# Expert stage of a two-block network: larger VectorE quotas per up round, and 20 instead of 4 gelu rows kept in SBUF

## What is computed

```python
def _peer(h, wq, keys, u, v):
    q = (hb @ wq).reshape(tc, PEER_HEADS, 2, PEER_HALF)
    s = jnp.einsum('thpk,hpnk->thpn', q, keys)
    s_top, i_top = lax.top_k(s, PEER_TOPK)
    cand = s_top[:, :, 0, :, None] + s_top[:, :, 1, None, :]
    best, pos = lax.top_k(cand.reshape(tc, PEER_HEADS, -1), PEER_TOPK)
    eid = jnp.take_along_axis(cid.reshape(tc, PEER_HEADS, -1), pos, -1)
    g = jax.nn.softmax(best)
    act = jax.nn.gelu(jnp.einsum('td,thed->the', hb, u[eid]), approximate=False)
    return jnp.einsum('the,thed->td', g * act, v[eid])
```

## Time and profile of the kernel before

| what | us |
|---|---|
| median of 3 runs | 3786.34 (3786.01 to 3790.39) |
| time of the profiled execution | 3789.86 |
| span of the profile | 3787.8 |
| up rounds of the changed stage, from the first gelu to the last | 489 to 1208.8 |
| pause until the first down product | 1208.8 to 1232.3 |
| down rounds | 1232.3 to 1791 |
| until the next stage starts | 1791 to 1807.8 |

### The profile page before, as it was taken

The page is one execution under the profiler, slowest core; times in us unless marked ns, Lnnn a source line. Parts: engine busy times, 40 slices in busy tenths (PEclk is TensorE's granted clock), DMA queues, the critical chain, the costliest instruction groups (busy, mean ns, idle before and its releaser), DMA issues. The chain is left out here.

```text
span 3787.8 us, 56067 instructions
## 1 busy us (share of the span) xinstructions
PE 3556.8 (94%) x21807; PEld 3153.1 (83%) x21807; DVE 2732.2 (72%) x5456; ACT 1689.3 (45%) x3029; POOL 395.3 (10%) x282
## 2 busy tenths in 40 slices
PE   7999999999997999998699999999997899989899
PEld 5777998999897877887577999998886888988798
DVE  4557366878786888888546797778887767766775
ACT  4344233555554333333434444443334535564554
POOL 0000000000454343343200000000000000000000
PEclk9999999999999999999899999999998999999999
DMA  5133366544899999998213575556665213442243
GB/s 229 63 132 133 114 244 253 186 168 167 324 352 346 332 390 365 369 381 310 85 51 145 184 231 186 167 184 229 251 242 187 112 72 146 181 169 90 83 173 139
DMA packets 181767, 773.02 MB, mean 204 GB/s; under 512 B 22976, under 2 KB 70592, under 8 KB 131584
## 3 DMA queue, kind: packets, MB, share of 16 engines
q1 hardware_dynamic: 144640, 635.20, 46.3%
q0 software_dynamic: 36864, 134.23, 9.4%
HBM read 699.38 MB, written 69.99 MB: 203 GB/s over the span
## 5 line engine op out<-in xcount | busy, mean ns | idle before, releaser
L2907 DVE TENSOR_TENSOR expert_ring_low<-expert_ring,expert_high 128x1024 fp32r<-128x1024 f32 x256 | 312.9, 1222 | 169.9 <-ACT expert_high L3236 166.6
L2192 ACT ACTIVATE expert_high<-expert_ring 128x1024 fp32r<-128x1024 f32 x256 | 270.6, 1057 | 211.3 <-PE ps L2119 211.3
L1922 DVE TENSOR_TENSOR expert_ring_low<-expert_ring,expert_high 128x1024 fp32r<-128x1024 f32 x256 | 311.7, 1219 | 70.7 <-ACT expert_high L2192 70.7
L3133 PE MATMUL ps<-hidden_high,expert_high 128*128 128x384 f32 x1024 | 353.7, 345 | 0.0
L3135 PE MATMUL ps<-hidden_high,expert_ring_low 128*128 128x384 f32 x1024 | 344.2, 336 | 0.0
L3134 PE MATMUL ps<-hidden_low,expert_high 128*128 128x384 f32 x1024 | 343.8, 336 | 0.0
L3236 ACT ACTIVATE expert_high<-expert_ring 128x1024 fp32r<-128x1024 f32 x256 | 270.0, 1055 | 118.0 <-PE ps L3170 112.5
L3424 POOL DMA_INDIRECT x<-in_peer_rows,spots x128 | 181.4, 1417 | 1107.7 <-DVE spots L2979 605.0
L2088 PE MATMUL ps<-peer_hT_high_peer,expert_high 128*128 128x256 f32 x1024 | 293.9, 287 | 0.6 <-DVE expert_ring_low L1922 0.5
L2090 PE MATMUL ps<-peer_hT_high_peer,expert_ring_low 128*128 128x256 f32 x1024 | 287.0, 280 | 0.0
L2089 PE MATMUL ps<-peer_hT_low,expert_high 128*128 128x256 f32 x1024 | 287.0, 280 | 0.0
(11 more groups left out here) (777 smaller groups left out, 9762.4 us busy)
## 6 DMA issues: line engine op xcount, KB each, us to landing
expert_ring<-in_peer_u SPq DMA_DIRECT2D x128, 1024.0 KB
expert_ring<-in_peer_v SPq DMA_DIRECT2D x128, 1024.0 KB
weight_ring<-in_ffn_w_up SPq DMA_DIRECT2D x22, 2048.0 KB, 7.5
weight_ring<-in_w_in SPq DMA_DIRECT2D x14, 2048.0 KB, 7.3
weight_ring<-in_w_mod SPq DMA_DIRECT2D x12, 2048.0 KB, 7.5
mod_slot<-in_w_mod SPq DMA_DIRECT2D x12, 2048.0 KB, 10.5
pair_weights<-pair_weights_out SPq DMA_DIRECT2D x24, 1024.0 KB
gelu_first<-gelu_out SPq DMA_DIRECT2D x62, 384.0 KB
```

Of the source, the lines that this page charges most:

```text
L1922: dve.tensor_tensor(piece(low, n), piece(raw, n), high[:, n % LEAD, :].bitcast(F32), ALU.subtract).then_inc(low_done, 1)
L2192: act.activation(high[:, n % LEAD, :], piece(raw, n), ACT.Identity).then_inc(high_done, 1)
L2907: dve.tensor_tensor(self.piece(G.e_low, n), self.piece(G.e_raw, n), G.e_high[:, n % LEAD, :].bitcast(F32), ALU.subtract).then_inc(self.S.l ...
L3133: pe.matmul(o, b[:, s], B.hs[0][:, c, 0:DW], start=(c == 0), stop=False)
```

## The change

The quotas become 3900 and 3300 ns; the down quota stays at 1700 ns. `STAY` = 20 rows of gelu stay in SBUF: 4 in the ring as before (`RING`), and the last 16 in a new tensor `ge_kept` of 24 KB a partition, which takes the place of the selection's buffers. The assertion on the end of the selection follows from it. The table's input buffer `w_in` moves to where the table's staging was, and with it the load of `x_last` moves from down round 24 to down round 124, behind a wait for the last use of that buffer. The down rounds begin 16 rows of keys earlier than before, and loads of gelu begin with down round 20.

```diff
@@ -2849,7 +2849,8 @@
 PARTS = PAIRS // PART
 LAG = PART + 2
 U_SLOTS, V_SLOTS = 3, 4
-EARLY_NS, TABLE_NS, DOWN_NS = 2600, 2300, 1700
+EARLY_NS, TABLE_NS, DOWN_NS = 3900, 3300, 1700
+STAY, RING = 20, 4
 GROW_AT = 40
 
 E_SIGNALS = (
@@ -2875,7 +2876,11 @@
 
     def expert(self, r):
 
-        return (r + N_KEYS - KEPT) % N_KEYS
+        return (r + N_KEYS - STAY) % N_KEYS
+
+    def gelu_at(self, e):
+
+        return self.B.ge_out[:, e % RING, :] if e < N_KEYS - STAY + RING else self.B.ge_kept[:, e - (N_KEYS - STAY + RING), :]
 
     def scores_of(self, g):
         k, n = divmod(4 * g, 2 * PEER_HEADS)
@@ -3044,8 +3049,8 @@
     def weigh(self, dve, r):
         S, B = self.S, self.B
         n, j = self.weights_of(r)
-        m = r // 4 - 1
-        if r < KEPT:
+        m = (r - STAY) // 4
+        if r < STAY:
             dve.wait_ge(S.gelu_done, self.expert(r) + 1)
         elif r % 4 == 0:
             dve.wait_ge(self.ge_landed[m % 2], 16 * (m // 2 + 1))
@@ -3053,7 +3058,7 @@
             dve.wait_ge(self.w_landed[n % 2], 16 * (n // 2 + 1))
         if r >= 1:
             dve.wait_ge(S.aw_split, r)
-        ge = B.ge_out[:, r, :] if r < KEPT else B.ge_in[:, m % 2, r % 4, :]
+        ge = self.gelu_at(self.expert(r)) if r < STAY else B.ge_in[:, m % 2, r % 4, :]
         w = B.w_in[:, n % 2, :, j * BLOCK:(j + 1) * BLOCK]
         dve.tensor_tensor(B.aw[:, :].rearrange("p (b t) -> p b t", t=BLOCK), ge.rearrange("p (b t) -> p b t", t=BLOCK), w,
                           ALU.mult).then_inc(S.aw_done, 1)
@@ -3084,7 +3089,7 @@
             left += EARLY_NS if r < TABLES_AT - 1 else TABLE_NS
             while left > 0:
                 left -= next(pieces, left)
-        assert at["selected"] < N_KEYS - 8
+        assert at["selected"] < N_KEYS - STAY
         for r in range(2):
             self.weigh(dve, r)
             self.split_weights(dve, r)
@@ -3238,9 +3243,9 @@
     def gelu(self, act, r):
         S, p = self.S, r // 2
         act.wait_ge(S.scored, r + 1)
-        if r % 2 == 0 and p >= 2:
+        if r % 2 == 0 and 2 <= p < (N_KEYS - STAY + RING) // 2:
             act.wait_ge(self.ge_stored[p % 2], 16 * (p // 2))
-        act.activation(self.B.ge_out[:, r % 4, :], self.G.ps[:, r % 3, 0:DW], ACT.Gelu).then_inc(S.gelu_done, 1)
+        act.activation(self.gelu_at(r), self.G.ps[:, r % 3, 0:DW], ACT.Gelu).then_inc(S.gelu_done, 1)
 
     def shares(self, act, g):
         S, B = self.S, self.B
@@ -3335,14 +3340,14 @@
     def load_ge(self, sp, m):
         B = self.B
         if m >= 2:
-            sp.wait_ge(self.S.aw_done, KEPT + 4 * (m - 1))
+            sp.wait_ge(self.S.aw_done, STAY + 4 * (m - 1))
         sp.dma_start(B.ge_in[:, m % 2, :, :], B.ge_dram[:, 4 * m:4 * m + 4, :]).then_inc(self.ge_landed[m % 2], 16)
 
     def load_w(self, sp, n):
         B = self.B
         if n >= 2:
             sp.wait_ge(self.S.aw_done, self.weights_end(n - 2))
-        first = (N_KEYS - KEPT, 0)[n > 0] if n == 0 else 8 * n - 8
+        first = self.expert(0 if n == 0 else self.weights_end(n - 1))
         size = 8 if 0 < n < W_LOADS - 1 else KEPT
         sp.dma_start(B.w_in[:, n % 2, :, 0:size * BLOCK],
                      B.w_dram[:, :, first * BLOCK:(first + size) * BLOCK].rearrange("b p n -> p b n")).then_inc(self.w_landed[n % 2], 16)
@@ -3356,7 +3361,7 @@
         for p in range(UNITS_U):
             sp.wait_ge(S.scored, UJ * (p + 1))
             self.load_unit(sp, p + E_SLOTS)
-            if UJ * p < N_KEYS - KEPT:
+            if UJ * p < N_KEYS - STAY:
                 sp.wait_ge(S.gelu_done, UJ * (p + 1))
                 sp.dma_start(B.ge_dram[:, UJ * p:UJ * p + UJ, :], B.ge_out[:, UJ * p % 4:UJ * p % 4 + UJ, :]).then_inc(
                     self.ge_stored[p % 2], 16)
@@ -3372,7 +3377,7 @@
             self.store_w(sp, b)
         sp.wait_ge(S.table_ready, DT)
         for b in range(2):
-            sp.wait_ge(self.ge_stored[b], 16 * (N_KEYS - KEPT) // (2 * UJ))
+            sp.wait_ge(self.ge_stored[b], 16 * (N_KEYS - STAY) // (2 * UJ))
         self.load_ge(sp, 0)
         self.load_ge(sp, 1)
         for b in range(2):
@@ -3384,17 +3389,18 @@
             sp.wait_ge(S.pv_done, r)
             if UNITS_U + q + E_SLOTS < 2 * UNITS_U:
                 self.load_unit(sp, UNITS_U + q + E_SLOTS)
-            if q % 2 == 1 and 2 <= q // 2 + 1 < (N_KEYS - KEPT) // 4:
-                self.load_ge(sp, q // 2 + 1)
+            if r % 4 == 0 and 2 <= (r - STAY) // 4 + 1 < (N_KEYS - STAY) // 4:
+                self.load_ge(sp, (r - STAY) // 4 + 1)
             n = (r - KEPT) // 8 + 2
             if r >= KEPT and (r - KEPT) % 8 == 0 and n < W_LOADS:
                 self.load_w(sp, n)
             if r == 24:
                 sp.dma_start(B.rows_w[:, :], B.ln_w.partition_broadcast(P)).then_inc(S.rows_landed, 16)
                 sp.dma_start(B.rows_b[:, :], B.ln_b.partition_broadcast(P)).then_inc(S.rows_landed, 16)
-                sp.dma_start(B.x_last[:, :], G.x_spill[:, SPARSE, :]).then_inc(S.x_landed, 16)
                 sp.dma_start(G.front.q.raw[:, :, :], G.front.q.src).then_inc(S.q_landed, 16)
             if r == N_KEYS - E_SLOTS:
+                sp.wait_ge(S.aw_done, self.weights_end(W_LOADS - 2))
+                sp.dma_start(B.x_last[:, :], G.x_spill[:, SPARSE, :]).then_inc(S.x_landed, 16)
                 G.ws.refill(sp, S.pv_done, (N_KEYS - E_SLOTS,))
         G.ws.refill(sp, S.pv_done, (N_KEYS, N_KEYS, N_KEYS))
         sp.wait_ge(S.dotted, PAIRS)
@@ -3491,11 +3497,12 @@
     B.shift = pick.take("best_shift", [P, PEER_HEADS, 16], F32)
     B.ex = pick.take("best_exp", [P, PEER_HEADS, 16], F32)
     B.sm = pick.take("best_sum", [P, PEER_HEADS, 2], F32)
-    B.w_in = room(96, 24).take("pair_weights_in", [P, 2, BLOCKS, 8 * BLOCK], F32)
+    B.w_in = room(16, 24).take("pair_weights_in", [P, 2, BLOCKS, 8 * BLOCK], F32)
     late = room(120, 12)
     B.aw = late.take("weighted", [P, DW], F32)
     B.ah = late.take("weighted_high", [P, 3, DW], F32R)
     B.al = late.take("weighted_low", [P, 3, DW], F32R)
+    B.ge_kept = room(96, 24).take("gelu_kept", [P, STAY - RING, DW], F32)
     B.table = room(127.5, 4.5).take("pair_table", [P, 3, DW], F32)
     B.ge_out = room(132, 6).take("gelu_out", [P, 4, DW], F32)
     few = room(138, 1.75)
```

## The result

The changed kernel takes 3820.10 us (median of 4 runs, 3817.92 to 3822.68) against 3786.18 us before; the ratio is 1.0088, with a 95% interval of 1.0076 to 1.0101. It is 33.9 us slower. Forecast were 19 us, 3805, with a range up to 3832.

A forecast was written before the change was run, and what follows sets the result against it. Up rounds with table work were taken as bound by a ring through DVE and ACT, down rounds by PE unless loads are late; +18 + 3 + 8 + 8 - 18 = +19 us on 3786.3 gave 3805, range 3775 to 3832.

The forecast's parts named there:

- the forecast's own: Whole kernel: the main forecast of 3805 us, with its own range of 3790 to 3818 and chance 0.50.
- rival 1: Up rounds: gathers choke them through the DMA engines or POOL's issues, +42 us, 3828; chance 0.18.
- The pause: Between up and down rounds: its chain of last group, store and table load stays the same, 0 +-3 us.
- The ring as bound: Up rounds with table work: a DVE and ACT dependency loop sets their length, leaving 3.24 us for DVE's pieces.
- Rival 2: Up rounds: short rounds repay long ones, so the added DVE work largely vanishes, 3760 to 3776; chance 0.15.
- Rounds with three pieces: Up rounds 55 to 127: 47 rounds each exceed DVE's free time by 0.38 us, +18 us.
- ACT's shares: Up rounds: ACT's gelu of eight dots waits for DVE in 12 rounds instead of two, net +8 us.
- Selection: Up rounds to 54: more exceed the free time, one exponential less falls by table rounds, net +3 us (0 to +8).
- Gathers in the up rounds: After a start both kernels pay, 53 rounds wait for rows at 393 GB/s, +8 us (0 to 31).
- POOL: Up rounds: 2.64 gather issues of 1.70 us each stay hidden while one takes under 2.23 us.
- Down rounds: Stalls after the 48th round go, and 1 to 3 us between the 24th and 48th: -18 us (-14 to -34).

The follow-up runs named there:

- e3: Changed kernel with quotas of 3900 ns in the first 31 up rounds and 2300 ns after, as before: 3772.71 us, ratio 0.9958.
- e5: Changed kernel with quotas of 3900 and 2500 ns, so never three sparse pieces in an up round: 3770.68 us, ratio 0.9957.
- e2: Kernel before, with 4 kept rows, given only the change's quotas of 3900 and 3300 ns: 3824.82 us, ratio 1.0091.
- e7: Changed kernel with gathers of 128 instead of 1024 columns for all rows of v and the first 96 of u: 3784.91 us, ratio 0.999.
- e4: Changed kernel with ACT's gelu of eight dot products one round later: 3809.43 us, ratio 1.0048.
- e1: Changed kernel with the quotas of before (2600 and 2300 ns), leaving only the 20 kept rows and their moves: 3785.84 us, ratio 0.9992.
- e10: Kernel before (4 kept rows) with quotas of 3900 and 2500 ns and ACT's gelu of eight dots one round later: 3773.48 us, ratio 0.9966.
- e11: Changed kernel (20 kept rows) with quotas of 3900 and 2500 ns and ACT's gelu of eight dots one round later: 3770.93 us, ratio 0.9957.
- e8: Changed kernel with quotas of 4400 and 2500 ns and ACT's gelu of eight dots one round later: 3783.46 us, ratio 0.9989.

## Why the prediction was right, and where it was off

**The sum.** Measured were +33.9 us, forecast +19. The measured time lies in the stated range, but 2 us past the forecast's own (3790 to 3818) and nearer rival 1 (3828) than 3805; and a sign of rival 1 appeared, DVE idle before dots for rows (20 times, 20.2 us). The up part grew by 46.4 us (forecast 37): 29 for the quotas, as forecast, and 17 for transfers, forecast 8. The pause added 4.2, forecast at nothing.

**The ring as bound: right.** That rounds of the table are set by a ring through DVE and ACT and not by PE, that 3.24 us are free in it, and that anything beyond is paid without repayment: e3 and e5 (never three pieces) keep 712.9 and 715.1 us, e2 and the change (three in most rounds) do not. Rival 2, the ring that absorbs, is out.

**Rounds with three pieces, and ACT's shares: right in sum.** Forecast were 18 and 8 us. The intervals of low parts show 5.76 to 5.90 for plain rounds of three, 7.45 for a share behind a third piece, and 6.08 to 6.15 for ten rounds of three that also hold the product `coefs` of eight gelu, which I hadn't counted. In e7, where rows are hardly late, the up part is 26.6 us longer than before. In it the start of the gathers is gone, which had cost 4.8 us before (the round with the wait of the earlier trace rows took 10.31 us), and its own dots still wait 2.2 us: 26.6 + 4.8 - 2.2 = 29 us for the quotas, selection included, the 18 + 3 + 8 of the forecast.

**Selection: right, though its row of the table says +8.5 against +3.** The +3 set the whole selection of the kernel before, up to round 82, against the shorter one after. But a part of the old one lies behind the 55th gelu, where the row ends: one exponential (the low part of 909.87 in the earlier trace rows came 8.57 us after the one before it, 3.06 over 5.51) and two rounds with large pieces, 1.29 and 0.34 over. With these 4.7 us the selection cost +3.8, and the row below it is +42.7 on the forecast's footing, not +38.0. Here is one of the rounds that two large pieces lengthen, DVE in the changed kernel:

```profile
698.97 1.23 DVE L2912 TENSOR_TENSOR expert_ring_low<-expert_ring,expert_high 128x1024 fp32r<-128x1024 f32 x1 [0.95 <-ACT expert_high L3241]
701.25 4.60 DVE L2974 TENSOR_REDUCE selected<-one_hot 128x128 f32<-128x2048 f32 x2
705.76 1.22 DVE L2912 TENSOR_TENSOR expert_ring_low<-expert_ring,expert_high 128x1024 fp32r<-128x1024 f32 x1
```

6.79 us from one low part to the next, 1.28 more than 5.51, as the prediction's 1.25.

**Gathers in the up rounds: the term that was mis-sized.** Forecast were 8 us; e7 gives 19.8, and on the forecast's footing, with the start that the kernel before pays too, 17. The rate wasn't the error. Windows of the changed kernel (columns as in rows 1) for the 67th to the 108th gelu and for the last 20 rounds:

```profile
885.00:1133.00 248.00, 225.04 (x1311) 213.87 (x1310) 223.34 (x251) 127.67 (x295) 162.84 (x108) 0.99 1.00 389
1133.00:1257.00 124.00, 111.56 (x644) 107.48 (x643) 109.71 (x123) 63.03 (x145) 81.60 (x54) 0.96 0.94 350
```

The 374 GB/s above are an average over parts that don't fill the engines. Where the DMA share is 1.00 the rate was 389, as good as the 393 assumed. There a round took 6.06 us, forecast 6.03, and 5.85 in e7, forecast 5.90: 8.6 us for 41 rounds. The rest lies where I had put nothing. Up to the 67th gelu the changed kernel loses 8.1 us to e7, not the same start as before: with three dots in a round several waits for rows follow one another. And the last 20 rounds lose 3.2, though at a share of 0.94 the engines weren't full all the time. On the forecast's footing that is 8.1 - (4.8 - 2.2) = 5.5 for the start, 8.6 and 3.2, 17.3 in all. The step that failed is that both kernels pay the start alike and that only the mean rate counts after it.

A late row also costs a second time, in PE's clock. After the round of 9.11 us at 1077.54, in which a dot waited 2.69 us for rows, PE had idled 3.66 us before its next work; its matmuls of 384 columns took 0.52 us instead of 0.33, and a round of three took 6.73 us instead of 5.80. The granted clock of this window is a mean of the two levels, 1.2 and 2.4 GHz:

```profile
1087.00:1099.00 12.00, 9.41 (x44) 9.44 (x45) 11.33 (x13) 6.12 (x14) 7.01 (x5) 0.72 0.86 299
```

The term lay between my bounds (0 and 31). Of the ceilings that the Trainium skill gives ("DMA: Bandwidth & Descriptors", section "Measured"), neither is what these stretches show: 425 GB/s for one core alone was not reached in any total here, 358 was passed.

**POOL: right to leave out.** Counted as in the prediction, with the idle time that nothing else explains, an issue took 1.80 us for v and 1.56 for u in the changed kernel (busy 1.62 and 1.40), under the 2.23 that would have counted. With DVE busy 88% instead of 80% the issue for v was thus 0.1 us dearer (that for u was cheaper, 1.56 against 1.69), not 0.53, and e7 needed as long for an eighth of the bytes.

**Down rounds: right, -18.6 against -18**, and in the places named: 16.0 us after the 48th round (330.1 before, 314.1 now), 1.6 between the 24th and 48th, 1.0 before.

**The pause: +4.2, forecast at nothing with +-3.** SP's issue of the table's two loads took 12.80 us instead of 7.00 before:

```profile
1220.91 7.00 SPq L3347 DMA_DIRECT2D pair_weights_in<-pair_weights  x2
```

```profile
1267.71 12.80 SPq L3352 DMA_DIRECT2D pair_weights_in<-pair_weights  x2
```

```profile
1246.31 6.32 SPq L3362 DMA_DIRECT2D pair_weights_in<-pair_weights  x2
```

The first row is of the kernel before, the second of the changed kernel, the third of e7. I had argued that its chain was the same and had not asked what the queues hold when it starts. In all three DVE's wait for the table ends about 2 us after this issue does. e7 has the quotas of the change and gathers of an eighth of the bytes, and there the pause is 27.8 us instead of 34.5. So the 4 us come with the bytes of the gathers that the plan leaves for this moment. In the other profiles, too, a long issue goes with a long pause: 6.01 and 27.9 us in e3, 8.88 and 32.0 in e2, 10.66 and 32.7 in e4.

**Open.** Why the last 20 up rounds still lose 3.2 us to the gathers at a share of 0.94, and why e4's profiled run gave its gain back to the gathers while its median did not.

## What to carry to other kernels

Before more work is given to an engine that looks 80% busy, read one period of the timeline and ask what sets its length: if the engine is part of a ring through others, only the idle time inside the ring is free, and work in units larger than that time is paid in every period. Count such free time in whole units: two pieces of 1.19 us fit into 3.24, three don't, and a quota of 2500 ns instead of 3300, with 3900 in the early rounds, turned 34 us of loss into 17 us of gain. Keeping data on chip pays only where its transfers were late; here they weren't, and 16 more kept rows gave nothing that can be told (e1, and e10 against e11). And where two limits lie close together, look at the stretches where work starts and ends, not only at the steady one: there this forecast failed.

## What was not expected of the hardware

Beside gathers of full rows SP issued more slowly: the same pair of table loads kept its sequencer 12.80 us in the changed kernel and 6.32 in e7, where the gathers bring an eighth of the bytes (7.00 in the kernel before). The time of an indirect gather's issue on POOL did not depend on the bytes: 194 issues took 294.6 us in e7, all but four of them with rows of 512 bytes, and 289.8 us with rows of 4 KB (the window of 811 to 1257 above). A wait costs more than its length, through PE's granted clock: 0.72 in the window of 1087 to 1099, after PE had idled 3.66 us, and 0.96 over the early rounds of e8, which took 15.5 us longer than with 3900 ns though PE idled only 10.1 of them. The window of e7 (columns as in rows 1):

```profile
809.00:1235.40 426.40, 394.31 (x2305) 374.51 (x2304) 391.90 (x447) 224.69 (x518) 294.63 (x194) 0.99 0.56 195
```
